# Second output projection ended row half by row half, the feed-forward norm's factor applied to the up products, and the last store in four parts

## The chip, the cores and the metric

The kernel runs on one core of one Trainium2 chip, in one launch, with inputs and outputs in device memory. The metric is the device time of one execution in microseconds (us), the median of several runs. The profile's trace counts time from the start of its span; TensorE, VectorE, ScalarE, GpSimd and SyncE are its PE, DVE, ACT, POOL and SP.

## The reference

The program is a small decoder of three parts over 256 tokens of width 1024: a recurrent layer and an attention layer, each with a squared-ReLU MLP, and then a block with three attention branches and a convolutional feed-forward part. Only the end of the last block matters here:

```
x = x + rmsnorm_2(merged @ w_out, norm_mix_post)             # second output projection
h = rmsnorm_2(x, norm_ffn_pre)
u = causal_depthwise_conv_2(h @ w_ffn_up, ffn_conv_w, ffn_conv_b)   # 2 x 2816 columns, 3 taps over tokens
y = (gelu(u[gate half]) * u[value half]) @ w_ffn_down
x = x + rmsnorm_2(y, norm_ffn_post)                          # the output

rmsnorm_2(x, g) = x * rsqrt(mean(x * x) + 1e-6) * g          # the mean is over the 1024 columns of a token
```

The factor `rsqrt(...)` is one number for each token, so `h @ w_ffn_up` is the same as `(x * g) @ w_ffn_up` with the factor applied afterwards to each token of the product.

## The kernel before

**Numbers.** Each float32 operand of a product is split into a high part that TensorE takes exactly and a low part; a product is three matmuls (high by high, high by low, low by high). Weights come in units of 1 MB, numbered 0 to 162, into four slots of `raw`. ScalarE writes the high part `whi` (L595), VectorE the low part `wlo` (L1424), each unit three units ahead of its use (`LEAD = 3`). ScalarE may write a slot only when TensorE is done with the unit that it held: `split(u)` waits for the step of unit u - 4 on the semaphore `s_step`. SyncE loads a unit when the low part of the unit that its slot held is done.

**Order.** Each engine has its own program, an order written out by hand, and runs it strictly from top to bottom. Engines meet on semaphores only. There is no planner.

**Second output projection.** Units 126 to 129 (`U_OUT2`), 256 rows of `w_out` each; the tokens are in two row halves t of 128 and the columns in two halves c of 512, so the product is four pieces (t, c) in PSUM banks 4 to 7. `layer_b` (L1068) goes through the units; `tokens` (L1039) does a unit for all four pieces in turn, and the last unit piece by piece: it signals `s_tok` after each of the first three pieces and `s_step` after the last. On ScalarE `unit_b(U_OUT2 + i)` for i = 0 to 3 (L948) stands ahead of that, each of them one split of unit 129 to 132. Then `squares` (L610, L619) squares and sums each piece as it comes. On GpSimd `roots` (L471) makes the factor of a row half from two sums, as `rstd`. `post` on VectorE (L1798) multiplies each piece by the factor and the gain into `xn` (L1805) and adds it to the residual `res` (L1807).

**Norm of the feed-forward part.** `norm(6, ...)`: ScalarE squares each finished piece of `res` (L619), GpSimd makes the roots, VectorE scales a row half into `xn` (L1432), TensorE transposes it (`norm_T`, L1076), ScalarE multiplies by the gain and rounds to the high part in `XA` (`norm_hi`, L652), VectorE makes the low part (`norm_lo`, L1466).

**Another way that the kernel has already.** Between an earlier projection and its MLP (`add_lift` L1436, `lift_hi` L629, `res_T` L1013, `first_up` L1021) the unscaled residual is transposed and multiplied by the gain, half of the columns at a time, and the up product begins before the norm's factor is known. The squares are taken behind that (`squares_res`, L645), and the factor is applied to the product at the end of the MLP. `roots_deferred` (L479) makes it.

**Feed-forward part.** 11 rounds j (`FFN_STEPS`), each with two up units (256 gate columns, 256 value columns; `unit_a`, `group`) and one down unit (`tokens`), in the order up(j + 1), down(j). ScalarE copies an up product from PSUM to `fu` (L964) and writes the last tap and the bias into `fc` (L965); VectorE adds the other two taps (L1822), ScalarE does the gelu (L977), VectorE the product (L1835), and the two make the high and low parts (L982, L1838). The last down unit is done piece by piece, then `squares`, `roots` and `post(1)` follow as above, and SyncE stores each row half (L448) after its two adds.

## Time and profile before

| | us |
|---|---|
| median of 3 runs | 1085.74 |
| lowest, highest | 1084.72, 1086.94 |
| the profiled execution | 1085.35 |
| its span in the trace | 1083.4 |
| mean granted clock of TensorE | 0.977 |

```profile
PE 1038.9 (96%) x6694; PEld 932.5 (86%) x6694; DVE 653.6 (60%) x893; ACT 570.0 (53%) x857; POOL 88.8 (8%) x106
...
PE   5999999999999988999999989999999979999997
...
PEclk9999999999999969999999999999999989999999
```

The first line is busy time, share of the span and number of instructions of each engine. The two others cut the span into 40 equal slices of 27 us; a digit is the busy share of TensorE, or its granted clock, in tenths, where 9 is 90% or more. The change touches the slices 32 to 34 (854 to 912 us), the rounds behind them and the last slice.

### The profile page before, as it was taken

How to read it: one execution, taken by the hardware profiler on the slowest of the kernel's cores; microseconds unless marked ns; L12 is line 12 of the kernel's file. 1: busy time of each engine (PE TensorE's matmuls, PEld its weight loads, DVE VectorE, ACT ScalarE, POOL GpSimd, SP SyncE). 2: the span in 40 equal slices, each digit the busy share in tenths (PEclk: the TensorE clock that was granted, in tenths of full speed). 3: DMA queues.
4: the chain of work that ended last, by engine and by line, in shares of the span. 5: the costliest groups of instructions: out<-in, count | busy, mean ns of one | idle time of the engine just before them, and what ended most of it. 6: DMA issues, size and time to landing. Idle time of an engine off the chain costs nothing. (4 is left out here: it accounts for less than half of the span.)

```text
span 1083.4 us, 16410 instructions
## 1 busy us (share of the span) xinstructions
PE 1038.9 (96%) x6694; PEld 932.5 (86%) x6694; DVE 653.6 (60%) x893; ACT 570.0 (53%) x857; POOL 88.8 (8%) x106
## 2 busy tenths in 40 slices
PE   5999999999999988999999989999999979999997
PEld 5988899989988855799999979988899869999996
DVE  5769655555567756465555564355564667667664
ACT  6597464444455545454444454356544457656652
POOL 3510010000000103230000000000002410000000
PEclk9999999999999969999999999999999989999999
DMA  9535595555526511475655537543334625655520
GB/s 313 191 128 187 176 319 177 191 192 194 189 83 241 186 40 58 139 236 189 194 194 179 184 116 216 160 123 111 117 117 156 208 68 197 205 190 183 194 79 39
DMA packets 117970, 180.40 MB, mean 167 GB/s; under 512 B 3113, under 2 KB 93577, under 8 KB 117913
## 3 DMA queue, kind: packets, MB, share of 16 engines
q1 hardware_dynamic: 116099, 174.16, 48.7%
q0 software_dynamic: 1696, 5.39, 1.4%
q8 instruction: 41, 0.67, 0.3%
q14 instruction: 16, 0.13, 0.0%
q10 hardware_dynamic: 118, 0.05, 0.0%
HBM read 178.48 MB, written 1.10 MB: 166 GB/s over the span
## 5 line engine op out<-in xcount | busy, mean ns | idle before, releaser
L999 PE MATMUL PS<-XA,whi 128*128 128x256 f32 x2576 | 476.2, 287 | 6.4 <-DVE XA L1475 4.4
L1424 DVE TENSOR_TENSOR wlo<-raw,whi 128x2048 fp32r<-128x2048 f32 x157 | 361.2, 2306 | 172.6 <-ACT whi L595 172.4
L999 PEld LDWEIGHTS PS<-XA,whi 128*128 128x128 f32 x2576 | 409.8, 194 | 16.5 <-issue 12.6
L595 ACT ACTIVATE whi<-raw 128x2048 fp32r<-128x2048 f32 x158 | 301.7, 1912 | 155.3 <-PE PS L1044 124.5
L999 PE MATMUL PS<-XA,wlo 128*128 128x256 f32 x1288 | 367.3, 285 | 0.0
L999 PEld LDWEIGHTS PS<-XA,wlo 128*128 128x128 f32 x1288 | 250.0, 194 | 0.0
L1044 PE MATMUL PS<-whi,XB 128*128 128x512 f32 x800 | 226.6, 391 | 1.0 <-DVE XB L1705 1.0
L1044 PEld LDWEIGHTS PS<-whi,XB 128*128 128x128 f32 x800 | 147.6, 188 | 30.0 <-issue 1.7
L1044 PE MATMUL PS<-wlo,XB 128*128 128x512 f32 x400 | 127.4, 390 | 0.0
L1044 PEld LDWEIGHTS PS<-wlo,XB 128*128 128x128 f32 x400 | 75.1, 188 | 15.9
L771 ACT ACTIVATE arena<-PS 128x256 f32<-128x256 f32 x64 | 24.2, 382 | 96.2 <-PE PS L999 95.7
L1044 PE MATMUL PS<-whi,XA 128*128 128x512 f32 x256 | 72.2, 390 | 1.6 <-DVE XA L1783 1.6
L1822 DVE SCALAR_TENSOR_TENSOR arena<-arena,fvec 128x256 f32<-128x256 f32 x88 | 38.8, 482 | 41.9 <-ACT arena L965 41.1
L1044 PEld LDWEIGHTS PS<-whi,XA 128*128 128x128 f32 x256 | 48.0, 188 | 11.6 <-issue 1.8
L1604 DVE SCALAR_TENSOR_TENSOR arena<-PS,arena 128x256 f32<-128x256 f32 x64 | 26.5, 420 | 42.3 <-ACT arena L771 42.3
L999 PE MATMUL PS<-XB,whi 128*128 128x256 f32 x256 | 46.5, 284 | 0.3 <-issue 0.3
L1044 PE MATMUL PS<-wlo,XA 128*128 128x512 f32 x128 | 42.0, 389 | 0.0
L600 ACT ACTIVATE arena<-PS 128x256 f32<-128x256 f32 x49 | 18.2, 380 | 44.4 <-PE PS L999 44.4
L999 PEld LDWEIGHTS PS<-XB,whi 128*128 128x128 f32 x256 | 39.9, 192 | 0.8 <-issue 0.8
L964 ACT ACTIVATE arena<-PS 128x256 f32<-128x256 f32 x44 | 16.7, 379 | 44.9 <-PE PS L999 44.9
L475 POOL TENSOR_SCALAR ss<-ss 128x1 f32<-128x1 f32 x12 | 5.5, 457 | 388.7 <-ACT arena L619 224.0
L999 PE MATMUL PS<-XB,wlo 128*128 128x256 f32 x128 | 36.2, 283 | 0.0
(209 smaller groups left out, 982.8 us busy)
## 6 DMA issues: line engine op xcount, KB each, us to landing
raw<-in_w_up SPq DMA_DIRECT2D x32, 1024.0 KB, 5.5
raw<-in_w_down SPq DMA_DIRECT2D x32, 1024.0 KB, 5.0
raw<-in_w_ffn_up SPq DMA_DIRECT2D x22, 1024.0 KB, 5.1
raw<-in_w_in SPq DMA_DIRECT2D x21, 1024.0 KB, 5.2
raw<-in_w_ffn_down SPq DMA_DIRECT2D x11, 1024.0 KB, 5.0
raw<-in_a_w_in SPq DMA_DIRECT2D x8, 1024.0 KB, 8.5
raw<-in_w_kv SPq DMA_DIRECT2D x8, 1024.0 KB, 6.1
raw<-in_w_mem_kv SPq DMA_DIRECT2D x4, 1024.0 KB, 5.1
```

Of the source, the lines that this page charges most:

```text
L475: link(pool.tensor_scalar(ss[:, 4 + t:5 + t], ss[:, 2 * t:2 * t + 1], ss[:, 2 * t + 1:2 * t + 2], EPS, ALU.add, ALU.add))
L595: act.activation(whi[:, s, :], raw[:, s, :], ACT.Copy).then_inc(s_hi, 1)
L600: act.activation(dst, PS[:, bank_of(g), 0:T], func, scale=scale).then_inc(s_evac, 1)
L771: act.activation(dst, PS[:, bank_of(g), 0:T], ACT.Relu).then_inc(s_relu, 1)
L964: act.activation(fu[:, f, 2:2 + T], v, ACT.Copy)
L999: ins = pe.matmul(PS[:, bank_of(g), 0:T], w[:, k, P * m:P * m + P], X[:, k0 + k, part, :], start=(i == 0 and part == 0 and w is hi), stop= ...
L1044: return pe.matmul(PS[:, bank + n * t + c, 0:width], X[:, k0 + k, part, P * t:P * t + P], w[:, k, c0 + 512 * c:c0 + 512 * c + width], star ...
L1424: dve.tensor_tensor(wlo[:, s, :], raw[:, s, :], whi[:, s, :].bitcast(F32), ALU.subtract).then_inc(s_lo, 1)
L1604: dve.scalar_tensor_tensor(dst, PS[:, bank_of(g), 0:T], 0.0, dst, ALU.max, ALU.mult).then_inc(s_evac, 1)
L1822: ins = dve.scalar_tensor_tensor(fc[:, f, :], fu[:, f, i:i + T], fvec[:, 0, c:c + 1], fc[:, f, :], ALU.mult, ALU.add)
```

## The change

- **TensorE.** The first two units of the second output projection are as before. Of the last two, row half 0 is finished first (unit 128 and unit 129 for both its pieces), then unit 128 for row half 1, whose end signals the unit's step, then piece (1, 0). Then it waits for the two adds of row half 0, transposes it from `res`, does piece (1, 1), waits for the add of piece (1, 0) and transposes its columns. The rest of row half 1 is transposed within the first up unit.
- **ScalarE.** The squares go to scratch (`junk`) in place of `xn` or PSUM. The residual's squares stand behind the lift. It copies the factor's row from PSUM to `rstd_row` and no longer copies the up products; the last tap is computed from `fu`.
- **VectorE.** `post` is in two steps: the product of a piece and the gain, once its square is taken, and one instruction that applies the factor and adds. It multiplies each up product by `rstd_row` into `fu`.
- **GpSimd.** The roots of this norm are deferred, into `dsc`.
- **TensorE again.** Behind the first up unit it waits for these roots and spreads them over all partitions with two matmuls against the identity.
- **SyncE.** It stores each of the four pieces after its add.

```diff
@@ -101,7 +101,7 @@
 XT_OF = [n + sum(d < n for d in DEFERRED) for n in range(7)]
-DS_MLP0, DS_KQV, DS_MLP1 = 0, 2, 4
+DS_MLP0, DS_KQV, DS_MLP1, DS_FFN = 0, 2, 4, 6
@@ -221,6 +221,7 @@
         mone = sb("mone", [P, 1])
+        rstd_row = sb("rstd_row", [P, T])
         PS = ctx.enter_context(nc.psum_tensor("PS", [P, 8, 512], F32))
@@ -264,6 +265,7 @@
         gpost = area(S[3], 2048).rearrange("p (t n) -> p t n", t=2)
+        junk = area(S[4], 2048).rearrange("p (t n) -> p t n", t=TT)
@@ -314,6 +316,7 @@
         s_gp = sem("post_gains")
+        s_yg, s_bc, s_row, s_fc = sem("gained"), sem("rstd_broadcast"), sem("rstd_row_ready"), sem("ffn_tap2")
         s_out = sem("out_written")
@@ -442,11 +445,12 @@
                     sp.dma_start(xn, A["mem_2"][0].rearrange("(t p) n -> p t n", p=P)).then_inc(s_mem, 16)
-            for t in range(TT):
-                sp.wait_ge(s_add, 4 * A_FFN + 2 * t + 2)
-                sp.dma_start(out[0, P * t:P * t + P, :], res[:, t, :]).then_inc(s_out, 16)
-            sp.wait_ge(s_out, 16 * TT)
+            for i, (t, c, _) in enumerate(pieces()):
+                sp.wait_ge(s_add, 4 * A_FFN + i + 1)
+                at = slice(512 * c, 512 * c + 512)
+                sp.dma_start(out[0, P * t:P * t + P, at], res[:, t, at]).then_inc(s_out, 16)
+            sp.wait_ge(s_out, 16 * 4)
@@ -560,7 +564,7 @@
             roots(SQ_POST[0])
-            roots(SQ_NORM[6])
+            roots_deferred(SQ_NORM[6], DS_FFN, mhalf)
             roots(SQ_POST[1])
@@ -952,18 +956,26 @@
-            squares(SQ_POST[0], None, product(A_OUT2, U_OUT2 + 3))
-            norm(6, res, [(XA, R_FFN)], added(A_OUT2))
-            def ffn_evac(u, g0, e, j):
+            def squares_tail(b, src, ready):
+                for i, (t, c, bank) in enumerate(pieces()):
+                    ready(i)
+                    v = PS[:, bank, :] if src is None else src[:, t, 512 * c:512 * c + 512]
+                    act.activation(junk[:, t, 512 * c:512 * c + 512], v, ACT.Square, scale=D ** -0.5, accum_out=ss[:, i:i + 1]).then_inc(s_ss, 1)
+            squares_tail(SQ_POST[0], None, product(A_OUT2, U_OUT2 + 3))
+            lift_hi(6, [(XA, R_FFN)], U_OUT2 + 3)
+            squares_tail(SQ_NORM[6], res, added(A_OUT2))
+            act.wait_ge(s_bc, 1)
+            act.activation(rstd_row[:], PS[:, 6, 0:T], ACT.Copy).then_inc(s_row, 1)
+            def ffn_tap2(g0, e, j):
...
                     f, c = 2 * e + m, e * 22 + 2 * j + m
-                    act.wait_ge(s_step, BEFORE(u) + m + 1)
-                    v = PS[:, bank_of(g0 + m), 0:T]
-                    act.activation(fu[:, f, 2:2 + T], v, ACT.Copy)
-                    act.activation(fc[:, f, :], v, ACT.Identity, scale=fvec[:, 1, c:c + 1],
-                                   bias=fvec[:, 1, 44 + c:45 + c]).then_inc(s_evac, 1)
+                    act.wait_ge(s_evac, g0 + m + 1)
+                    act.activation(fc[:, f, :], fu[:, f, 2:2 + T], ACT.Identity, scale=fvec[:, 1, c:c + 1],
+                                   bias=fvec[:, 1, 44 + c:45 + c]).then_inc(s_fc, 1)
@@ -971,16 +983,16 @@
                     act.wait_ge(s_fl, j)
-                ffn_evac(u, G_FFN + 4 * j, 0, j)
+                ffn_tap2(G_FFN + 4 * j, 0, j)
                 split(u + 1 + LEAD)
...
                 act.activation(fc[:, 0:2, :], fc[:, 0:2, :], ACT.Gelu_apprx_tanh).then_inc(s_gelu2, 1)
-                ffn_evac(u + 1, G_FFN + 4 * j + 2, 1, j)
+                ffn_tap2(G_FFN + 4 * j + 2, 1, j)
                 if j:
...
                 act.activation(XB[:, 2 * (j % 2):2 * (j % 2) + 2, 0, :], fc[:, 0:2, :], ACT.Copy).then_inc(s_fh, 1)
-            squares(SQ_POST[1], None, product(A_FFN, N_UNITS - 1))
+            squares_tail(SQ_POST[1], None, product(A_FFN, N_UNITS - 1))
@@ -1018,7 +1030,7 @@
-            def first_up(u, g, n, product):
+            def first_up(u, g, n, second_half):
@@ -1026,7 +1038,7 @@
                     if k == 2:
-                        res_T(1, product, 4)
+                        second_half()
                     pe.wait_ge(s_xlo, NORM_HI[n] + k + 1)
@@ -1130,7 +1142,8 @@
                 u0, g0, p0 = mlp_base(layer)
-                first_up(u0, g0, *((2, A_ROUT) if layer == 0 else (4, A_O)))
+                n, product = (2, A_ROUT) if layer == 0 else (4, A_O)
+                first_up(u0, g0, n, lambda: res_T(1, product, 4))
@@ -1376,17 +1389,70 @@
                     branch(b, k)
-            layer_b(U_OUT2, XA, ready=lambda i: pe.wait_ge(s_ml, i // 2 + 1))
-            norm_T(6)
+            for i in range(2):
+                have(U_OUT2 + i)
+                pe.wait_ge(s_ml, 1)
+                tokens((U_OUT2 + i) % SLOTS, W2, 2, XA, 2 * i, 4, 2, i == 0, False)
+            def out2_piece(i, t, c):
+                s = (U_OUT2 + i) % SLOTS
+                hi, lo = W2(whi, s), W2(wlo, s)
+                for k in range(2):
+                    for part_, w in ((0, hi), (0, lo), (1, hi)):
+                        ins = pe.matmul(PS[:, 4 + 2 * t + c, :], XA[:, 2 * i + k, part_, P * t:P * t + P],
+                                        w[:, k, 512 * c:512 * c + 512], start=False,
+                                        stop=(i == 3 and k == 1 and part_ == 1), skip_group_check=True)
+                return ins
+            def token_T(t, half):
+                for k in range(4 * half, 4 * half + 4):
+                    ins = pe.transpose(resT(k)[:, P * t:P * t + P], res[:, t, P * k:P * k + P], ident[:])
+                return ins
+            pe.wait_ge(s_ml, 2)
+            have(U_OUT2 + 3)
+            for t in range(TT):
+                for c in range(2):
+                    ins = out2_piece(2, t, c)
+                if t == 1:
+                    ins.then_inc(s_step, 1)
+                out2_piece(3, t, 0).then_inc(s_tok, 1)
+                if t == 0:
+                    out2_piece(3, t, 1).then_inc(s_tok, 1)
+            pe.wait_ge(s_add, 4 * A_OUT2 + 2)
+            for half in range(2):
+                token_T(0, half)
+            out2_piece(3, 1, 1).then_inc(s_step, 1)
+            pe.wait_ge(s_add, 4 * A_OUT2 + 3)
+            token_T(1, 0).then_inc(s_xnT, 1)
+            def ffn_second_half():
+                pe.wait_ge(s_add, 4 * A_OUT2 + 4)
+                token_T(1, 1).then_inc(s_xnT, 1)
...
                 u = U_FFN if j == 0 else U_FFN + 2 + 3 * (j - 1)
-                unit_a(u, G_FFN + 4 * j, xready=NORM_HI[6] if j == 0 else None)
+                if j == 0:
+                    first_up(u, G_FFN, 6, ffn_second_half)
+                    pe.wait_ge(s_rstd, ROOTS[SQ_NORM[6]] + TT)
+                    for t in range(TT):
+                        ins = pe.matmul(PS[:, 6, P * t:P * t + P],
+                                        dsc[:, DS_FFN + t:DS_FFN + t + 1].to_broadcast([P, P]), ident[:],
+                                        start=(t == 0), stop=(t == 1), skip_group_check=True)
+                    ins.then_inc(s_bc, 1)
+                else:
+                    unit_a(u, G_FFN + 4 * j)
                 unit_a(u + 1, G_FFN + 4 * j + 2)
...
                 have(u)
+                if j == 0:
+                    pe.wait_ge(s_row, 1)
                 pe.wait_ge(s_fl, j + 1)
@@ -1798,16 +1864,37 @@
                 dve.wait_ge(s_gp, 32)
-                for t in range(TT):
-                    dve.wait_ge(s_rstd, ROOTS[SQ_POST[n]] + t + 1)
-                    for c in range(2):
-                        y, v = (x[:, t, 512 * c:512 * c + 512] for x in (xn, res))
-                        link(dve.scalar_tensor_tensor(y, PS[:, 4 + 2 * t + c, :], rstd[:, t:t + 1],
-                                                      gpost[:, n, 512 * c:512 * c + 512], ALU.mult, ALU.mult))
-                        dve.tensor_tensor(v, v, y, ALU.add).then_inc(s_add, 1)
+                def gained(i):
+                    t, c, bank = pieces()[i]
+                    dve.wait_ge(s_ss, 4 * SQ_POST[n] + i + 1)
+                    at = slice(512 * c, 512 * c + 512)
+                    dve.tensor_tensor(xn[:, t, at], PS[:, bank, :], gpost[:, n, at], ALU.mult).then_inc(s_yg, 1)
+                def add(i):
+                    t, c, _ = pieces()[i]
+                    at = slice(512 * c, 512 * c + 512)
+                    dve.wait_ge(s_yg, 4 * n + i + 1)
+                    if c == 0:
+                        dve.wait_ge(s_rstd, ROOTS[SQ_POST[n]] + t + 1)
+                    dve.scalar_tensor_tensor(res[:, t, at], xn[:, t, at], rstd[:, t:t + 1], res[:, t, at], ALU.mult,
+                                             ALU.add).then_inc(s_add, 1)
+                gained(0)
+                gained(1)
+                add(0)
+                add(1)
+                gained(2)
+                gained(3)
+                add(2)
+                add(3)
             post(0)
-            norm(6, res, [(XA, R_FFN)], late=U_OUT2 + 3 + LEAD)
+            for k in range(KT):
+                dve.wait_ge(s_xhi, NORM_HI[6] + k + 1)
+                dve.scalar_tensor_tensor(XA[:, k, 1, :], resT(k), vecs[:, R_FFN + k:R_FFN + k + 1],
+                                         XA[:, k, 0, :].bitcast(F32), ALU.mult, ALU.subtract).then_inc(s_xlo, 1)
+            split(U_OUT2 + 3 + LEAD)
             for k in range(4):
@@ -1815,7 +1902,7 @@
-                dve.wait_ge(s_evac, g0 + 2)
+                dve.wait_ge(s_fc, g0 + 2 - G_FFN)
                 for i in range(2):
@@ -1828,6 +1915,13 @@
                 for e in range(2):
+                    if j == 0 and e == 0:
+                        dve.wait_ge(s_row, 1)
+                    for m in range(2):
+                        g = G_FFN + 4 * j + 2 * e + m
+                        dve.wait_ge(s_step, BEFORE(u + e) + m + 1)
+                        dve.tensor_tensor(fu[:, 2 * e + m, 2:2 + T], PS[:, bank_of(g), 0:T], rstd_row[:], ALU.mult)\
+                           .then_inc(s_evac, 1)
                     split(u + e + LEAD)
```

## Rows read from the trace of the kernel before

**Rows 1.** Busy time by stage, with clock and DMA share: feed-forward seam, body and end.

```profile
873.40:886.60 13.20, 6.55 (x28) 5.01 (x26) 7.51 (x12) 5.78 (x17) 3.84 (x8) 0.78 0.05 16
886.60:911.80 25.20, 25.15 (x193) 25.18 (x194) 20.18 (x30) 18.34 (x28) 0.00 (x0) 0.91 0.45 152
911.80:1064.60 152.80, 152.80 (x1082) 144.18 (x1081) 103.58 (x117) 88.53 (x116) 0.00 (x0) 1.00 0.48 161
1072.80:1083.40 10.60, 2.74 (x13) 1.93 (x11) 5.51 (x8) 2.06 (x6) 1.72 (x4) 0.78 0.24 99
```

**Rows 2.** Chain of waits from 854 us on: start us, us, what it was.

```profile
854.04 19.32 PE PS L1044 x84
873.38 0.70 ACT arena L619 x2
875.22 0.76 DVE arena L1805
881.58 3.90 PE PS L1081 x16
885.51 0.48 ACT XA L664
886.65 25.17 PE PS L999 x192
917.28 11.51 PE PS L999 x96
```

**Rows 3.** Timeline of ScalarE at the end of the second output projection: start, length, what.

```profile
870.72 1.92 ACT L595 ACTIVATE whi<-raw 128x2048 fp32r<-128x2048 f32 x1 [3.52 <-PE PS L1044]
872.54 0.57 ACT L619 ACTIVATE arena<-PS 128x512 f32<-128x512 f32 x1
```

**Rows 4.** TensorE's stretches: us, busy (instructions), granted clock, DMA.

```profile
638.00:639.00 1.00, 0.68 (x3) 0.69 0.00 0
880.00:881.00 1.00, 0.00 (x0) 0.86 0.00 0
886.60:890.90 4.30, 4.25 (x20) 0.50 0.00 0
890.00:891.00 1.00, 1.00 (x6) 0.52 0.09 16
1078.00:1079.00 1.00, 0.00 (x0) 0.85 0.58 238
```

**Rows 5.** Timeline of TensorE ahead of 638 us.

```profile
634.13 1.09 PE L1081 MATMUL PS<-ident,arena 128*128 128x128 f32 x8 [1.51 <-DVE arena L1432]
```

**Rows 6.** Timeline of the seam into the second MLP: transposes, lift, squares, root.

```profile
449.70 1.03 PE L1018 MATMUL PS<-ident,res 128*128 128x128 f32 x8
450.77 0.84 ACT L641 ACTIVATE XA<-PS,vecs 128x256 fp32r<-128x256 f32 x2 [4.05 <-PE PS L1018]
462.56 0.62 ACT L649 ACTIVATE arena<-res 128x512 f32<-128x512 f32 x1
466.63 0.56 POOL L485 TENSOR_TENSOR dsc<-ss,mone 128x1 f32<-128x1 f32 x1
```

**Rows 7.** Two VectorE lines: duration ns min/median/max, first and last start, forms.

```profile
L1443 DVE TENSOR_TENSOR res<-res,PS x8: 686/688/689, 121.0 to 452.1; 128x512 f32<-128x512 f32 x8
L1604 DVE SCALAR_TENSOR_TENSOR arena<-PS,arena x64: 406/418/425, 135.0 to 622.1; 128x256 f32<-128x256 f32 x64
```

**Rows 8.** Timeline of the last down unit, the last square and the last add.

```profile
1068.77 0.69 DVE L1838 TENSOR_TENSOR XB<-arena,XB 128x512 fp32r<-128x512 f32 x1 [0.70 <-ACT XB L982]
1069.48 0.84 PE L1044 MATMUL PS<-whi,XB 128*128 128x512 f32 x3
1075.58 0.60 ACT L619 ACTIVATE arena<-PS 128x512 f32<-128x512 f32 x1 [0.67 <-PE PS L1044]
1079.64 0.69 DVE L1807 TENSOR_TENSOR res<-res,arena 128x512 f32<-128x512 f32 x1
```

**Rows 9.** DMA issues: what, engine, count, KB each, median us to landing.

```profile
out<-res SPq DMA_DIRECT2D x2, 512.0 KB, 2.6
```

## Prediction

> **What bounds the kernel now.** The table of stages comes first [rows 1]. In the feed-forward part, 911.8 to 1064.6 us, TensorE is busy for all of 152.8 us at full clock, while VectorE is busy for 103.6 and ScalarE for 88.5. That stage ends with TensorE, and no work on another engine shortens it. The two stages beside it are different: from 873.4 to 886.6 TensorE is busy for 6.55 of 13.2 us at a mean clock of 0.78, and in the last 10.6 us for 2.74. The change touches both of these and the seam into the long stage.
>
> The chain of waits [rows 2] says what fills the hole. The second output projection ends near 876; before that ScalarE takes the squares of a row half, GpSimd the root, VectorE two instructions for each of four pieces, then the scaled rows, the transposes from 881.58 to 885.48, one ScalarE and one VectorE instruction, and the up product starts at 886.65. Its first 192 matmuls take 25.17 us; 144 of them at the steady step of 0.12 us (11.51 us for 96) are 17.27, so unit 131 (the second half of them starts there, after 48) began at 911.81 - 17.27 = 894.54. That instant is my yardstick for the middle: from unit 131 on everything is TensorE at its own pace.
>
> The clock is read third [rows 4]. TensorE stopped at 876.06; its granted clock fell to 0.5 (1.2 GHz) at about 880.7 and was back at 1.0 (2.4 GHz) at about 891. Over 886.6 to 890.9 there are 20 matmuls, which at 0.12 us each would need 2.4 us: 1.85 us lost.
>
> **The middle, new order.** TensorE issues one 512-column matmul per 0.228 us (the 84 of the chain's row take 19.32 us less the last one's own tail; 854.04 is the start) [rows 2]. Both orders have the same 96. Numbering them from 0, the new order ends the third weight unit (U_OUT2 + 2) with matmul 83, not 71, and the piece of row half 0, columns 512 on, with 71; the third piece ends with 89. So the steps: pieces (0,0) and (0,1) are complete at 869.2 and 870.6, the unit's step is signalled at 873.33, and the third piece is done at 874.7.
>
> Row half 0 is thus ready 2.7 us earlier than before, and the intent would be met if ScalarE squared it there. But ahead of the squares ScalarE still has the split of unit 132 into its high part, the fourth of `unit_b(U_OUT2 + i)`. It overwrites the slot of unit 128 = U_OUT2 + 2, so it waits for that unit's step. In the trace it is the row at 870.72 with 3.52 us of waiting on TensorE, 0.12 us after matmul 71 ended, and the first square follows 1.82 us later at 872.54 [rows 3]. That step now comes 12 matmuls later. Queued behind the waiting split are all four squares, the lift and, through them, GpSimd, VectorE and TensorE. So:
> - split at 873.45, first square 875.27, second 875.9 (step 0.63, they no longer wait for pieces).
> - From the start of the second square to VectorE's use of the root: 873.38 to 875.22, 1.84 us [rows 2]. VectorE adds row half 0 from 877.75; the two gain products (0.69 each, as another product of PSUM and SBUF [rows 7]) fit before it. Two adds in SBUF, taken at 0.69 each too, overlapping by 0.05: done at 879.1.
> - TensorE now waits for both adds before it transposes, with its last piece behind the transposes. It has nothing from 874.7 to 879.15, 4.45 us, and then eight transposes and six matmuls. In the trace the clock went down 4.7 us after a stop, and at the end of the kernel 3.2 us after one (the fourth square's start at 1075.58 marks it, the fall is at about 1078.7); at 638.4 it fell some 4 us after a gap of only 1.5 us, with transposes in between [rows 4, 5]. I take it low here: transposes 1.6 us, as 16 took 3.90 [rows 2]; matmuls of 512 columns at low clock are not in these rows, so 0.43 each, twice the low-clock step of 256 columns (4.25 us over 20). The piece ends at 883.5.
> - Fourth square 883.5, VectorE's add of piece (1,0) 1.84 later at 885.35, done 886.05; four transposes, 1.1 us at low clock (at full clock eight take 1.07, from 449.70 to ScalarE's start at 450.77 [rows 6], so four 0.67); then ScalarE and VectorE and the up product, as from 885.51 to 886.65, 1.14 us. Start 888.3, or 1.65 us later than before.
>
> If the clock stays high instead, the same steps give 881.5, 884.1, 884.8 and 885.95: 0.7 us earlier than before. That is the lower bound.
>
> **The factor on the up products.** The squares of the residual leave the path ahead of the up product and come back behind it: TensorE does unit 130, then waits for the deferred root, makes two 128-column broadcasts, and only then goes on to unit 131. After 12 matmuls (2.56 us at low clock: 890.9) come the second half's transposes (1.1: 892.0), the last four lifted tiles (two per 1.03 us, the last pair 0.87: 893.9), four squares and two roots. The first layers have just that tail: squares at 462.56, last root at 466.63 + 0.56, 4.63 us [rows 6]. That gives 898.5, and two broadcasts, each like one transpose with its end (0.27 to 0.48), some 0.35: unit 131 starts near 898.8, 4.3 us later than the 894.54 of before. Unit 130 itself (48 matmuls 5.76 us, transposes, 1.85 for the clock) is through by about 896.3, so about 2.2 us are a pure stall. At full clock throughout it would be 885.95 + 1.44 + 0.67 + 1.87 + 4.63 + 0.35 = 894.9, plus 0.4. What a 2.2 us stall does to the clock is open: at 638.4 a 1.5 us gap and transposes were enough for a fall [rows 4, 5]. A fall costs 1.85 as above, or nothing; I take half, 0.9.
>
> GpSimd's root waits: `roots_deferred` works on the same two instructions a row half, priced above. Moving ScalarE's evacuation of 44 groups to VectorE adds 44 multiplications, 0.42 us each as [rows 7] have it for one PSUM and one SBUF operand: 1.7 us in each 16.98 us round, where VectorE is idle for a third of the time [rows 1]. They stand before the split of unit u + 3, which has two units (over 11 us) to spare. Cost nothing; what covers it is TensorE. The tightest place is the last down unit: its low part of the hidden rows is ready at 1068.77 + 0.69 = 1069.46, and its first matmul is the third of the row at 1069.48, 1069.94 [rows 8]. The evacuation now takes 0.42 on VectorE where ScalarE's copy took 0.28, some 0.2 later, leaving 0.25. Were it missed the price is the miss itself, under 0.3.
>
> **The end.** Here nothing is held in front of ScalarE. Gain products of row half 0 run before its root is there, so behind the root at 1074.7 (two pieces, 2.73 us, ahead of that of half 1) only one VectorE instruction per piece is left. Adds of half 0 to 1076.0; gain products of half 1 at 1075.95 and 1076.6; its root comes at 1077.4 (1075.58 plus 1.84), adds to 1078.7. Before, the last add ended at 1079.64 + 0.69 = 1080.33 [rows 8]: 1.6 us gained. The last store carries half the bytes: the DMA share of 0.24 over 10.6 us is 2.5 us for the two stores of before [rows 1], 1.3 for 512 KB, so 0.65 for 256. The span ended 3.07 us after the last add; it should be 2.4. The value is 0.7, the bounds 0 (the four stores get in one another's way) and 0.7. Together 2.3, at least 1.6.
>
> The Trainium skill speaks against the four stores: "DMA: Bandwidth & Descriptors", "Rules for kernel authors", wants many small transfers made into one, and "Anatomy of one DMA" gives each a fixed 2.0 us beside its bytes. With that fixed part paid four times in a row the last store would land no earlier than before and the end would gain about 0 to 0.7 instead of 2.3, which would put the whole at 1090. The row shows 2.6 us to landing for a 512 KB store [rows 9], less than the page's 3.2; two stores 2.8 us apart cannot show whether they overlap.
>
> **Sum.** The profiled execution took 1085.35 us (span 1083.4 and 1.95 around it), 0.39 below the median of 1085.74, inside the spread of the three (1084.72 to 1086.94); I add half of that. 1085.35 + 4.3 + 0.9 - 2.3 + 0.2 = 1088.4, rounded 1088.3. Without the second fall of the clock 1087.4, with it 1089.3.
>
> **Rivals.**
> 1. *The clock or the cover is kinder.* The clock is still high when TensorE takes up the last piece at 879.15 and low only later. The piece then ends at 881.5, the up product starts at 886.2 to 886.9, unit 131 starts at 896.7 to 897.3: middle 2.2 to 2.8, sum 1085.5 to 1086.0, no change. For it: after 876.06 the clock stood 4.7 us. Against: 3.2 us at the end, and the new gap is 4.45.
> 2. *The clock never falls.* Middle 0.4, sum 1083.7, barely faster. Against it: every long hole in these rows has a fall.
> 3. *It works as meant: the square of row half 0 is not held.* Should the split of unit 132 not hold the squares, squares start at 869.3 and 870.6, adds of half 0 end at 873.8, TensorE has no gap at all before the transposes (874.5), the piece ends at 876.9, the up product starts at 881.3 and unit 131 at 890.3 to 891.8. The middle gains 2.7 to 4.3 and the sum is 1079.0 to 1080.5. This decides at one place: whether the first square starts before or after 873.4. Against it: program order on ScalarE, and the row at 870.72.
> 4. *More is lost* behind the stall, where splits of units 133 and 134 now start some 8 us later than at 889.35 on ScalarE and a late one could stop TensorE. I find unit 133's low part done near 903.5 and needed at 910.3. Price 1 to 3 us, 1090 to 1092.
>
> **How the numbers follow.** Held squares with a low clock, my forecast: 0.62; rival 1: 0.20; rival 2: 0.07; rival 3: 0.06; rival 4: 0.05. What a measurement here can tell from no change is about 0.2%, 2.2 us: slower begins at 1087.9 and faster at 1083.6. The forecast's own range is 1086.8 to 1089.8. With the second fall it lies beyond 1087.9, without it (1087.4) a little more than half the time does not reach it; I count 0.50 of its 0.62 as slower, the rest as same. Slower 0.50 + 0.05 = 0.55, same 0.12 + 0.20 + 0.03 = 0.35, faster 0.10. The range 1085.0 to 1090.8 leaves out rivals 2 and 3 and half of rival 4.
>
> **What would show it.** In the changed trace: the split on ScalarE ahead of the first square waits on TensorE until about 873.4, and the first square starts at 875.3 (right) or near 869.3 (rival 3). TensorE is idle for about 4.4 us between the third piece and the transposes. The up product starts at 888; unit 130 is followed by a wait on GpSimd's root of about 2 us; unit 131 starts at 898.8. Rounds stay 16.98 us. From TensorE's last matmul to the end of the span 7.3 us become about 5. The forecast is wrong if the first square is early, if the clock row between 877 and 891 shows 1.0, or if TensorE waits for a split or an evacuation in the rounds.

## The result, and the profile after

The changed kernel takes 1088.99 us (median of 15 runs) where the kernel before, timed beside it, takes 1086.82 (15 runs): ratio 1.0021, 95% interval 1.0014 to 1.0029. One of the 15 executions of the changed kernel took 1691.95 us at a mean granted clock of 0.557, and the ratio leaves it out. So the change costs 2.3 us, 1.5 to 3.2. The forecast was 1088.3 against 1085.74, a ratio of 1.0024, and slower, by over 0.2%, the likeliest; the measured 0.21% stands on that line.

Line numbers of the changed kernel are not those of before: the tail of the second output projection is L1403, the transposes L1411, the first up unit L1045, the broadcast L1443, the squares L964, the up products L1011 and the down products L1056.

The table of stages of the changed kernel has the same columns as [rows 1].

```profile
874.90:888.10 13.20, 6.09 (x22) 4.41 (x22) 5.02 (x8) 4.33 (x9) 1.72 (x4) 0.74 0.05 17
888.10:900.74 12.64, 10.17 (x62) 9.76 (x61) 6.12 (x14) 5.86 (x16) 1.76 (x4) 0.73 0.11 35
900.74:1071.10 170.36, 170.36 (x1226) 161.69 (x1226) 131.37 (x178) 93.17 (x96) 0.00 (x0) 1.00 0.50 165
1077.00:1087.60 10.60, 4.76 (x21) 3.59 (x20) 5.41 (x8) 2.76 (x8) 1.73 (x4) 0.96 0.27 99
```

The 13.2 us from 874.90 on have 6.09 us of TensorE in them, where [rows 1] had 6.55 in the 13.2 us from 873.40 on; and behind them there is a second thin stretch, up to the start of unit 131 at 900.74, at a mean clock of 0.73. The rounds are dense as before, the end has a shorter hole. The chain of waits (start us, us, what; "..." marks lines left out) gives the order of events:

```profile
855.58 11.14 PE PS L1056 x48
866.73 8.17 PE PS L1403 x36
...
874.98 1.91 ACT whi L599
876.90 1.16 ACT arena L964 x4
...
879.21 1.43 DVE res L1880 x2
...
880.67 1.97 PE PS L1411 x8
882.64 2.57 PE PS L1403 x6
...
885.24 0.70 ACT arena L964 x2
...
889.71 2.90 PE PS L1045 x12
892.61 0.87 PE PS L1411 x4
...
895.40 2.46 ACT arena L964 x8
...
900.02 0.71 PE PS L1443 x4
900.74 17.28 PE PS L1011 x144
918.01 5.47 PE PS L1056 x24
```

The stage began 1.54 us later here than in [rows 2] (855.58 for 854.04), though the code above is the same; so I compare distances from that start. The reader is to see three things. First, behind 36 matmuls of the new tail stands not a square but a split, L599 at 874.98. (TensorE does six more matmuls, the third piece, while that split runs.) Second, two rounds of square, root and add, one after the other (from 876.90 and from 885.24), each followed by TensorE. Third, a long chain between the first 12 matmuls of the up product (889.71) and the broadcast (900.02): transposes, lift, squares, roots. ScalarE's timeline shows who waits for whom:

```profile
874.98 1.91 ACT L599 ACTIVATE whi<-raw 128x2048 fp32r<-128x2048 f32 x1 [6.24 <-PE PS L1403]
876.80 0.58 ACT L964 ACTIVATE arena<-PS 128x512 f32<-128x512 f32 x1
```

[Rows 3] has 3.52 us of waiting ahead of the split at 870.72; here it is 6.24, and the first square is behind it, at 876.80. TensorE's own line for the transposes has the gap that follows:

```profile
880.67 1.97 PE L1411 MATMUL PS<-ident,res 128*128 128x128 f32 x8 [4.43 <-DVE res L1880]
```

Of the clock (columns as in [rows 4]):

```profile
880.67:885.30 4.63, 4.53 (x14) 0.50 0.00 0
885.30:888.60 3.30, 0.66 (x4) 1.00 0.00 0
...
889.71:895.50 5.79, 5.79 (x27) 0.50 0.01 3
```

It fell at about 878.4, 2.2 us after TensorE's last matmul of the third piece ended at 876.25. It is at 1.2 GHz for the transposes and the last piece, back at 2.4 in a hole where it serves four transposes, and at 1.2 again for the first 5.8 us of the up product, where [rows 4] had 4.3. The changed end, its DMA and TensorE's wait for the root:

```profile
1075.19 0.69 DVE L1932 TENSOR_TENSOR XB<-arena,XB 128x512 fp32r<-128x512 f32 x1 [0.70 <-ACT XB L994]
...
1081.80 0.60 ACT L964 ACTIVATE arena<-PS 128x512 f32<-128x512 f32 x1 [0.67 <-PE PS L1056]
...
1083.63 1.41 DVE L1880 SCALAR_TENSOR_TENSOR res<-arena,rstd,res 128x512 f32<-128x512 f32 x2
```

```profile
out<-res SPq DMA_DIRECT2D x4, 256.0 KB, 2.1
```

```profile
PE PS L1443 <- POOL dsc L489: 1.3, 1, 1.3
```

The low part of the hidden rows for the last down unit is there at 1075.19 + 0.69 = 1075.88, and TensorE does not wait for it: the matmul that needs it starts at 1076.14, 0.26 us later. From the fourth square's start to the end of the span it is 1081.80 to 1087.5, 5.7 us; [rows 8] and the span of before give 1075.58 to 1083.4, 7.8.

A measure for the middle that the kernels share is the stretch from the first matmul of the second output projection to the first matmul of the first down unit. Before: 911.81 - 854.04 = 57.8 us. After: 918.01 - 855.58 = 62.4, 4.7 more. The end gives back 2.1. That is 2.6 for the stages that the change touches, and 2.3 by the ratio of the times. (The two profiled executions themselves lie 4.1 us apart, 1089.43 and 1085.35; 1.5 of it is the later start of the stage.)

### The profile page after: what moved, and what is told of

Its sections match the earlier page's. It is cut to its first block and busy times, and to the rows that moved or that the text cites. A ratio compares the mean times of both kernels' runs of the same rounds, so it can differ in the third digit from the quotient of the medians.

```text
span 1087.5 us, 16424 instructions
## 1 busy us (share of the span) xinstructions
PE 1040.9 (96%) x6698; PEld 932.6 (86%) x6698; DVE 664.8 (61%) x935; ACT 558.1 (51%) x814; POOL 88.5 (8%) x106
## 5 line engine op out<-in xcount | busy, mean ns | idle before, releaser
L1011 PE MATMUL PS<-XA,whi 128*128 128x256 f32 x2544 | 466.8, 285 | 4.4 <-DVE XA L1541 3.3
L1011 PEld LDWEIGHTS PS<-XA,whi 128*128 128x128 f32 x2544 | 401.3, 193 | 14.5 <-issue 9.6
L599 ACT ACTIVATE whi<-raw 128x2048 fp32r<-128x2048 f32 x158 | 301.3, 1910 | 144.1 <-PE PS L1056 107.9
L1011 PE MATMUL PS<-XA,wlo 128*128 128x256 f32 x1272 | 361.0, 284 | 0.0
L1011 PEld LDWEIGHTS PS<-XA,wlo 128*128 128x128 f32 x1272 | 245.0, 193 | 0.0
L1056 PE MATMUL PS<-whi,XB 128*128 128x512 f32 x800 | 226.7, 391 | 1.0 <-DVE XB L1771 1.0
L1056 PEld LDWEIGHTS PS<-whi,XB 128*128 128x128 f32 x800 | 147.6, 188 | 30.2 <-issue 1.7
L1056 PE MATMUL PS<-wlo,XB 128*128 128x512 f32 x400 | 127.4, 390 | 0.0
L1056 PEld LDWEIGHTS PS<-wlo,XB 128*128 128x128 f32 x400 | 75.1, 188 | 15.9
L775 ACT ACTIVATE arena<-PS 128x256 f32<-128x256 f32 x64 | 24.2, 383 | 96.2 <-PE PS L1011 95.7
L1056 PE MATMUL PS<-whi,XA 128*128 128x512 f32 x224 | 63.0, 390 | 1.6 <-DVE XA L1849 1.6
L1056 PEld LDWEIGHTS PS<-whi,XA 128*128 128x128 f32 x224 | 42.0, 188 | 10.4 <-issue 1.8
L1011 PE MATMUL PS<-XB,whi 128*128 128x256 f32 x256 | 46.5, 284 | 0.7 <-issue 0.7
L977 ACT ACTIVATE arena<-arena,fvec 128x256 f32<-128x256 f32 x44 | 25.9, 596 | 37.5 <-DVE arena L1923 37.5
L1011 PEld LDWEIGHTS PS<-XB,whi 128*128 128x128 f32 x256 | 39.9, 192 | 1.2 <-issue 1.2
L604 ACT ACTIVATE arena<-PS 128x256 f32<-128x256 f32 x49 | 18.2, 381 | 43.8 <-PE PS L1011 43.8
L1923 DVE TENSOR_TENSOR arena<-PS,rstd_row 128x256 f32<-128x256 f32 x44 | 18.2, 420 | 32.1 <-PE PS L1011 29.0
L1056 PE MATMUL PS<-wlo,XA 128*128 128x512 f32 x112 | 36.5, 389 | 0.0
L1011 PE MATMUL PS<-XB,wlo 128*128 128x256 f32 x128 | 36.2, 283 | 0.0
```

Of the source, the lines that this page charges most:

```text
L599: act.activation(whi[:, s, :], raw[:, s, :], ACT.Copy).then_inc(s_hi, 1)
L604: act.activation(dst, PS[:, bank_of(g), 0:T], func, scale=scale).then_inc(s_evac, 1)
L775: act.activation(dst, PS[:, bank_of(g), 0:T], ACT.Relu).then_inc(s_relu, 1)
L977: act.activation(fc[:, f, :], fu[:, f, 2:2 + T], ACT.Identity, scale=fvec[:, 1, c:c + 1], bias=fvec[:, 1, 44 + c:45 + c]).then_inc(s_fc, 1)
L1011: ins = pe.matmul(PS[:, bank_of(g), 0:T], w[:, k, P * m:P * m + P], X[:, k0 + k, part, :], start=(i == 0 and part == 0 and w is hi), stop= ...
L1056: return pe.matmul(PS[:, bank + n * t + c, 0:width], X[:, k0 + k, part, P * t:P * t + P], w[:, k, c0 + 512 * c:c0 + 512 * c + width], star ...
```

## The experiments

In each kernel the measure of the middle, the stretch just defined, is read off the chain of one profiled execution; the time is the ratio to the kernel before, timed on the same chip. The 95% interval of a ratio is 1.1 to 1.9 us to either side.

**1. Is it ScalarE's split that holds the squares?** `split_later`: the split of unit 132 goes behind the third square.

```diff
-            for i in range(4):
+            for i in range(3):
                 unit_b(U_OUT2 + i)
...
                 for i, (t, c, bank) in enumerate(pieces()):
+                    if i == 3 and between is not None:
+                        split(between)
                     ready(i)
...
-            squares_tail(SQ_POST[0], None, product(A_OUT2, U_OUT2 + 3))
+            squares_tail(SQ_POST[0], None, product(A_OUT2, U_OUT2 + 3), between=U_OUT2 + 3 + LEAD)
```

> The changed kernel with one thing moved: ScalarE's split of unit 132 stands behind the third square of the second output projection, not ahead of the first. My theory (the split waits for the step of unit 128 and holds the squares): the first square starts about 6 us earlier, TensorE's gap of 4.4 us before the transposes goes, unit 131 starts 2.7 to 4.3 us earlier than in the kernel before, and with the end's 2.1 us the whole is 4.8 to 6.4 us faster than before (about 7 to 9 faster than the changed kernel). Rival (the delay comes from doing the last piece behind row half 0's adds and transposes, in whatever order ScalarE works): the split's place is worth under 1.5 us, and the kernel stays within 0.2% of the kernel before or slower.

Measured: 1082.67 us, 0.9964 (0.9953 to 0.9976), 3.9 us faster than before and, by the medians, 6.3 faster than the changed kernel. ScalarE's first square and then the chain:

```profile
871.65 0.60 ACT L966 ACTIVATE arena<-PS 128x512 f32<-128x512 f32 x1 [2.10 <-PE PS L1405]
```

```profile
856.40 11.13 PE PS L1058 x48
...
883.95 2.90 PE PS L1047 x12
...
893.85 1.22 PE PS L1445 x4
895.07 18.15 PE PS L1013 x144
913.23 5.47 PE PS L1058 x24
```

The first square starts 15.25 us behind the stage's start; in the changed kernel it is 21.22. The up product starts at 27.55 us (was 34.13), and the gap of 4.4 us ahead of the transposes is gone. One instruction's place in ScalarE's order was worth 6 us of the time (5.6 of the middle): the theory holds, the rival is out. But the middle is 56.8 us, 0.9 less than before, not the 2.7 to 4.3 less that I expected. The broadcast took 1.22 us instead of 0.71, and the 144 matmuls behind it 18.15 instead of 17.28: the granted clock was down a second time, 0.50 from 894.4 to 896.4, right behind a wait of 2.2 us for the root.

**2. What does TensorE's wait for the root cost?** `broadcast_later`, on the changed kernel: the wait and the two broadcasts stand behind unit 131.

```diff
                 if j == 0:
                     first_up(u, G_FFN, 6, ffn_second_half)
-                    pe.wait_ge(s_rstd, ROOTS[SQ_NORM[6]] + TT)
...
                 else:
                     unit_a(u, G_FFN + 4 * j)
                 unit_a(u + 1, G_FFN + 4 * j + 2)
+                if j == 0:
+                    pe.wait_ge(s_rstd, ROOTS[SQ_NORM[6]] + TT)
...
```

> The changed kernel with TensorE's wait for the deferred root and its broadcast behind unit 131, not between units 130 and 131. Theory (TensorE stalls 1.3 us there, by the changed kernel's trace, and VectorE's late start on the first round has over 4 us of cover): 1.0 to 1.5 us faster than the changed kernel, about 1 us slower than before. Rival (the first round's chain on ScalarE and VectorE, which starts with the factor's row, becomes late for the first down unit): no gain, and a new wait of TensorE on the low part of the hidden rows near 915.

Measured: 1087.07 us, 1.0009 (0.9998 to 1.0019), by the ratios 1.3 us faster than the changed kernel, which the intervals do not set apart from nothing. The middle is 61.1 us, 1.3 less. The number is the one expected of the theory, but the trace gives it another source. The chain, and TensorE's waits (engine, line waited for, us in total, times, longest):

```profile
891.04 4.30 PE PS L1045 x36
...
914.64 5.72 PE PS L1056 x24
```

```profile
PE PS L1011 <- DVE arena L1924: 1.1, 1, 1.1
PE PS L1056 <- DVE XB L1933: 0.3, 1, 0.3
```

The wait of 1.3 us for the root is gone, and two others have come in its place, 1.1 us for the first evacuation and 0.3 us for the first low part of the hidden rows: that is the rival. The chain now runs through the first round on VectorE and ScalarE up to the first down unit. What made the middle shorter is unit 130, whose code is the same: its second transposes and last 36 matmuls took 0.48 and 4.30 us here, 0.87 and 5.25 in the changed kernel, since the clock was back 2.9 us behind the start of the up product and not 5.8. So this run does not show what the wait for the root costs; it shows that the broadcast's move alone trades one wait for two.

**3. The two moves together**, `both_later`.

> Both moves together. Theory: with the split moved the up product starts near 881 (trace time of the kernel before) and unit 130 is through about 2.4 us ahead of the root, so the broadcast's move is worth more here: 7 to 9 us faster than before, 0.992 to 0.9935. Rival (clock): the holes that are left (2.6 and 1.1 us around the last transposes) still bring the clock down, and 2 us of that do not show. Rival (first round late): TensorE waits at the first down unit for what the broadcast's move took, and this kernel equals the one with the split's move alone.

Measured: 1083.08 us, 0.9963 (0.9950 to 0.9977), 4.0 us faster than before where 7 to 9 were expected, and no better than `split_later`. The stage's first and last line of the chain:

```profile
856.37 11.15 PE PS L1058 x48
...
910.87 5.71 PE PS L1058 x24
```

The middle is 54.5 us, 2.3 less than `split_later`, but by the times the two cannot be told apart. The second rival is seen at work, with the same two waits as in experiment 2: TensorE waits 1.1 us for the first evacuation, since its two banks are needed again by unit 132, and 0.3 us for the first low part. The 2.3 us of the profile are about the wait for the root (2.2) and the second fall (0.9, and 0.8 in the broadcasts) less these waits (1.4). I cannot say by these runs why 2.3 us of a profile do not show in the medians; they are of 12 and of 6 runs that spread over 2 us or more.

**4. The end alone**, `end_only` (the kernel before with the last norm in two steps and four stores) and `end_two_stores` (the same with two stores).

> The kernel before with the change's end alone: the last norm's gain product ahead of its root and four stores. Theory (the end gains 2.1 us whatever the middle does): 2.1 us faster than before, 0.998. Rival (four stores pay their fixed cost in turn): 0 to 0.7 us faster.

> The kernel before with the gain product ahead of the last norm's root, and the two stores as before. Theory: 1.6 us faster than before, and the four stores of end_only are worth the other 0.5 to 0.7. Rival (four stores are worth nothing): the same as end_only.

Measured: 0.9968 (0.9957 to 0.9979) and 0.9986 (0.9974 to 0.9997), 3.5 and 1.5 us. In their profiles the stretch from the fourth square to the end of the span is 5.7 and 6.3 us for the 7.8 of before; the product ahead of the root is thus worth 1.5 and the four stores 0.6. The profiles bear out the theory. The times do not measure the share of the four stores: 2.0 us lie between the two ratios, with intervals of 1.2 us to either side, and 0.6 rests on one profiled execution of each. The ratio of `end_only` lies below it by more than its interval's half (0.998 was expected, 0.9979 is the interval's end), and I have no cause for it: its middle is the 57.7 us of before.

**5. What does the clock cost in the gap?** `gap_filled`, on the changed kernel: matmuls whose results are never read, written where the transposes write later.

```diff
+            def fill(n, bank):
+                w = W8(whi, U_FFN % SLOTS)
+                for i in range(n):
+                    pe.matmul(PS[:, bank, :].rearrange("p (a n) -> p a n", a=2)[:, :, P:T], w[:, 0, 0:P],
+                              w[:, 1, 0:T], start=True, stop=True, skip_group_check=True)
+
+            have(U_FFN)
+            fill(32, 3)
             pe.wait_ge(s_add, 4 * A_OUT2 + 2)
```

> The changed kernel with 32 more matmuls of 256 columns on TensorE between the third piece and the wait for row half 0's adds (3.8 us of the 4.4 us gap; their results lie where the transposes write later and are never read). Theory (the fall of the clock in that gap doubles the transposes, the last piece and part of the up product): granted clock 1.0 until the last piece is done, the up product starts about 2 us earlier, 2 to 4 us faster than the changed kernel, so 1 us slower to 2 us faster than before. Rival (only the holes cost, the clock does not): within 0.5 us of the changed kernel.

Measured: 1089.3 us, 1.0026 (1.0014 to 1.0039): nothing gained. The chain, and the clock in three stretches:

```profile
854.44 11.14 PE PS L1056 x48
...
879.53 1.09 PE PS L1411 x8
...
886.93 2.90 PE PS L1045 x12
...
897.94 18.76 PE PS L1011 x144
916.70 5.47 PE PS L1056 x24
```

```profile
874.50:879.50 5.00, 4.43 (x35) 1.00 0.01 2
...
886.93:892.80 5.87, 5.87 (x32) 0.60 0.01 3
...
896.20:900.00 3.80, 2.77 (x17) 0.79 0.85 276
```

The steps are the theory's and the time is the rival's. The clock stayed up through the gap, the transposes took 1.09 us and the last piece 1.4 (1.97 and 2.57 in the changed kernel), and the up product started 1.64 us earlier, at 32.49 us for 34.13. Then it fell all the same, within the four transposes behind the next gap (1.08 us at 884.69, 0.67 in the changed kernel), stayed low into the first up unit, and fell once more behind the root. TensorE waited 1.8 us for the root instead of 1.3, and the 144 matmuls took 18.76 us for 17.28. The middle is 62.3 us, as without the filler.

**6. Was that second fall the wait's doing?** `gap_filled_broadcast` adds one thing to `gap_filled`, the broadcast between the two halves of unit 131.

> gap_filled with the broadcast between the two halves of unit 131. In gap_filled the clock stayed up through the last piece, the up product came 1.6 us earlier, and TensorE then waited 1.8 us for the root and ran 144 matmuls in 18.8 us in place of 17.3: the gain was given back. Theory (that wait brought the clock down a second time): with it gone the stretch to the first down unit is 59 us in place of 62.3, about 3 us faster than the changed kernel, 1 us faster than before. Rival (the two holes around the second transposes bring it down in any case): the clock is low in the first up units still, the wait's 1.8 us alone is gained, 60.5 us.

Measured: 1085.6 us, 0.9992 (0.9979 to 1.0005), the middle:

```profile
853.71 11.14 PE PS L1056 x48
...
898.04 14.39 PE PS L1011 x120
912.44 5.47 PE PS L1056 x24
```

58.7 us, where the theory had 59 and the rival 60.5. 120 matmuls in 14.39 us are 0.12 each, full speed. Without the wait there is no second fall in this profiled execution, and with the same filler the kernel is 3.7 us faster by the ratios. There is no kernel with this place of the broadcast and no filler, so the filler's own share of the 3.7 is not shown. In the first up unit the clock was low as before, so the rival is right that it falls around the second transposes in any case, and wrong in its 60.5: the second fall went with the root's wait.

**7. A version that beats both.** `first_round_early` has both moves, the broadcast between the halves of unit 131, and the splits of units 133 and 134 ahead of the wait for the factor's row on ScalarE and VectorE. `first_round_filled` adds fillers around the second transposes. `one_split_early` puts the splits of unit 134 back. From the diff of `one_split_early` against the changed kernel:

```diff
+            fill(19, 3)
             pe.wait_ge(s_add, 4 * A_OUT2 + 3)
             token_T(1, 0).then_inc(s_xnT, 1)
+            fill(7, 3)
...
                     if j == 0 and e == 0:
+                        split(U_FFN + LEAD)
                         dve.wait_ge(s_row, 1)
```

> Both moves, and the first round made ready: the broadcast stands between the two halves of unit 131, and the splits of units 133 and 134 on ScalarE and VectorE stand ahead of the wait for the factor's row. Theory (with both moves TensorE waited 1.1 us for the first evacuation and 0.3 us for the first low part of the hidden rows): those two waits go, 1.3 us faster than both moves, 6 to 7 us faster than before, 0.994. Rival (splits ahead delay the factor's row by 2 to 4 us): the wait of 1.1 us stays or grows.

> The same as first_round_early, with 19 matmuls of 256 columns on TensorE between the last piece and the wait for the add of piece (1, 0), and 7 behind that piece's transposes; results never read. Theory: the clock stays at 1.0 through the first up unit, 1 to 2.5 us faster than first_round_early, 7.5 to 9 us faster than before. Rival (the fillers end behind the waits that they stand before, since TensorE's gap was 2.8 and 1.2 us): no gain or 0.5 us slower.

> first_round_filled with only the splits of unit 133 ahead of the factor's row, those of unit 134 back where the changed kernel has them. Theory (in first_round_filled TensorE waited 0.8 us for the first evacuation, which VectorE gave late behind two splits of 2.3 us): that wait goes, the stretch from the second output projection's start to the first down unit falls from 52.7 to 51.9 us, about 8 us faster than before, 0.9925. Rival (the first low part of the hidden rows becomes late instead, by more than 0.8 us): the same or slower, with a wait ahead of the first down unit.

| kernel | median us | ratio to before | 95% interval | middle us |
|---|---|---|---|---|
| first_round_early | 1079.90 | 0.9951 | 0.9934 to 0.9969 | 54.4 |
| first_round_filled | 1079.01 | 0.9932 | 0.9917 to 0.9946 | 52.7 |
| one_split_early | 1078.80 | 0.9922 | 0.9906 to 0.9937 | 51.7 |

Both waits of `both_later` are gone in `first_round_early`, but its middle is 54.4 us, not the 53.2 that I expected, and it is 5.3 us faster than before and not 6 to 7: the clock was low for longer in its first up unit, with the same code up to there (36 matmuls in 5.41 us, 4.31 in `both_later`). With fillers the clock stays up and one wait is back, because VectorE has two splits ahead of the first evacuation:

```profile
PE PS L1015 <- DVE arena L1942: 0.8, 1, 0.8
```

Taking one of them out removes it:

```profile
856.18 11.13 PE PS L1058 x48
...
883.71 1.67 PE PS L1047 x12
...
907.85 5.47 PE PS L1058 x24
```

The 12 first up matmuls take 1.67 us (2.90 in the changed kernel). This kernel is 8.5 us faster than before (6.8 to 10.2) and by its median, taken on another chip, 10.2 faster than the changed one. It does the same computation and 26 matmuls that nobody reads. The step from `first_round_early` to `first_round_filled` is 1.7 us of the middle in one profiled execution each; the two ratios' intervals overlap, so the times do not set it apart.

## Why the prediction was right

Distances are from the stage's start, after against before or against the step as predicted (854.04 taken off).

- *The split of unit 132 holds the squares.* Predicted: first square at 875.27, 21.23 us. Measured 21.22. Shown by experiment 1 as well, not only by the trace.
- *TensorE's gap.* 4.45 predicted, 4.43 measured. *The clock low for transposes and last piece*: 883.5 - 854.04 = 29.5; measured 29.6. The clock fell 2.2 us after TensorE's stop, sooner than the 4.7 and 3.2 of [rows 4]; with a gap of 4.45 those rows did not decide between this and my rival 1, and that it came out my way is in part luck. Its price up to the up product, 2.35 us in my two sums (888.3 and 885.95), is 1.64 in `gap_filled` (where the four transposes of piece (1, 0) then ran at the low clock, and in the changed kernel at the high one). As a gain of the whole it is refuted: what is taken there is given back at the root. My rival 2, no fall at all with a middle of 0.4, could therefore not have come from a filled gap alone.
- *Up product.* Predicted 34.26, measured 34.13. One of my signs of being wrong was a granted clock of 1.0 between 877 and 891, and it was 1.0 from 885.3 to 888.6. The four transposes in there took 0.67 us, not 1.1; the steps ahead of them took 0.25 more than I had, so the start hardly moved.
- *The deferred root.* Predicted 44.5 (898.5), measured 44.4. Unit 131 then started 45.16 behind the stage's start, 44.8 predicted: the broadcasts took 0.71 us, not 0.35. The two matmuls are four instructions in the trace, where I priced one transpose with its end. The middle is 4.7 for 4.3.
- *The stall at the root* was 1.3 us, not 2.2, as the clock came back 1.5 us later and unit 130 was slower: as priced, it moves time between two terms and not their sum.
- *A second fall* was counted at half of 1.85 us. In the profiled execution of the changed kernel it did not happen; in `split_later` (0.9 us, and 0.5 in the broadcast) and `gap_filled` (1.5) it did. So it does happen, but the 0.9 was no part of this profile's 4.7, and no run shows how often the changed kernel has it.
- *The end.* 2.3 predicted, 2.1 measured: the product ahead of the root 1.5 for 1.6, the stores 0.6 for 0.7. The Trainium skill's rule against small transfers ("DMA: Bandwidth & Descriptors", "Rules for kernel authors") did not decide here: the stores of a row half are issued some 0.7 us apart and each lands 2.1 us after its issue, so two are in flight at once and neither lands later for it, and four stores were the better end by 0.6 us. The fit that the Trainium skill gives ("DMA: Bandwidth & Descriptors", "Anatomy of one DMA") makes 2.6 us of 256 KB, an estimate by its figures. It is stated there for transfers issued by GpSimd, and these are SyncE's, which took 2.1. My last sign had 7.3 us from TensorE's last matmul to the end of the span become about 5; the trace before has 7.9 there and the one after 5.7, the same 2.1 less.
- *The rounds.* 16.98 us each, as before (11.51 + 5.47), although VectorE's work rose; no wait in them, and the last down unit's cover held, at 0.26 us for the 0.25 forecast.
- *Rival 3*, the intent: with the one move that it names the time was 1082.67, not 1079.0 to 1080.5. Its up product (881.3, 27.3 us) was right at 27.55; its unit 131, 37.8 at the latest, was wrong at 38.7, and the 144 matmuls behind it took 0.9 more. The second fall accounts for these 0.9 and for 0.5 in the broadcasts; I had priced it only in my own case. *Rival 4* did not occur in the changed kernel. Its like came in experiments 2 and 3, where TensorE waited 0.3 us for a low part that stood behind those splits, and in `first_round_filled`, 0.8 us for an evacuation behind them.
- *The total, and what was luck in it.* The terms are 4.3 + 0.9 - 2.3 = 2.9, and measured in the profiles they are 4.7 + 0 - 2.1 = 2.6: the fall that did not come made up for the broadcasts and the end, each a little worse than forecast. The sum as written gives 1088.45 and not 1088.3. And the kernel before had its median at 1086.82 in 15 runs, 1.1 above the 1085.74 that I started from, so 1088.99 is near 1088.3 with a start that was too low.

## What to carry to other kernels

Before work is reordered on one engine, look at what the *other* engines have in program order ahead of the instruction that should profit: a wait there on a step that the reordering delays (here the slot of a weight unit) takes the gain and more. Where a stall is removed, name what is late next and move that as well; here three waits stood one behind the other, and with the first gone the middle was 0.9 us shorter than before, with all of them gone 6.1. And look at what stands behind a filler against the fall of the clock: in `gap_filled` a later wait and a later fall took back the 1.6 us that it gave.

## What was not expected of the hardware

- The stage began anywhere between 853.3 and 856.4 us in kernels whose code is the same up to there: in the twelve profiled executions at 853.30, 853.54, 853.71, 854.04, 854.32, 854.44, 854.91, 854.96, 855.58, 856.18, 856.37 and 856.40. The granted clock falls at other places in the early, thin stages from one execution to the next: from 432 to 438 it is 0.72 in the kernel before and 1.00 in the changed one, from 416 to 424 it is 1.00 and 0.60. That is more than the change itself is worth, so two profiled executions can only be compared stage by stage.
- Inside a stage the same holds on a smaller scale. Behind the start of the up product the clock stayed at 1.2 GHz for 5.8 us in the changed kernel and for 2.9 in `broadcast_later`, for 2.8 in `both_later` and 5.8 in `first_round_early`, each pair with the same code up to there. That is 1.3 to 1.5 us of the middle, and differences of that size between two profiled executions need a second sign beside them.
- The granted clock can come back in a hole: it was 1.0 from 885.3 to 888.6, where TensorE did four transposes in 3.3 us, behind a stretch in which it was busy throughout at 1.2 GHz, and low again when the next work came.
